# A residual block on one core: thirteen instead of nine column groups of the feed-forward projection are begun ahead, one product of each is kept in DRAM, and the operands made from the second half of the tokens come in another order

## The reference, cut to what matters

```python
x = x + rms_norm(mix, norm_post_mix[l])          # mix: two branches, merged, projected

h = rms_norm(x, norm_pre_ffn[l])
f = (jax.nn.silu(h @ w_ffn_gate[l]) * (h @ w_ffn_up[l])) @ w_ffn_down[l]
x = x + rms_norm(f, norm_post_ffn[l])
```

## Time and profile before

| what | value |
| --- | --- |
| median of 3 runs | 1701.26 us (1701.11 to 1701.61) |
| profiled execution, its own time | 1703.39 us |
| profiled execution, span from first to last instruction | 1701.3 us |
| PE busy | 1626.9 us (96%) |
| POOL busy | 1305.1 us (77%) |
| DVE busy | 1002.7 us (59%) |
| mean granted TensorE clock | 0.98 |

### The profile page before, as it was taken

How to read it: one execution, slowest core, us unless ns; L and a number is a source line. 1 busy time by engine, 2 the same in 40 slices (tenths; PEclk the granted TensorE clock), 3 DMA queues, 4 the chain that set the end, 5 groups by cost and what they waited for, 6 DMA issues and landing times.

```text
span 1701.3 us, 24101 instructions
## 1 busy us (share of the span) xinstructions
PE 1626.9 (96%) x7328; PEld 1333.4 (78%) x7328; DVE 1002.7 (59%) x1148; ACT 567.9 (33%) x1065; POOL 1305.1 (77%) x1300
## 2 busy tenths in 40 slices
PE   8899999999999999999999967999999999999995
PEld 6677888888888778888888756788888887888884
DVE  5799736642177997666522679787555557215503
ACT  4577535442236775255322323101001013102000
POOL 5699976777787999867777755887777776778874
PEclk8999999999999999999999988999999999999997
DMA  4433433233354343522333451232222222734531
GB/s 145 118 99 111 118 104 88 74 96 98 94 149 118 103 112 108 169 75 79 93 93 97 139 183 44 84 103 87 69 62 68 74 62 60 239 95 139 190 110 59
DMA packets 113357, 178.89 MB, mean 105 GB/s; under 512 B 12672, under 2 KB 41600, under 8 KB 113280
## 3 DMA queue, kind: packets, MB, share of 16 engines
q1 hardware_dynamic: 90816, 135.97, 27.8%
q10 hardware_dynamic: 22464, 41.95, 7.4%
HBM read 157.42 MB, written 14.16 MB: 101 GB/s over the span
## 4 chain that ended last, share of the span: by engine, by line
PE 77%; POOL 12%; DVE 5%; issue 4%; ACT 2%; ACTq 0%; DMA 0%; POOLq 0%; SPq 0%; DVEq 0%
PE ps L730 11%; PE ps L732 11%; PE ps L731 11%; PE ps L961 8%; PE ps L963 8%; PE ps L962 7%; POOL w_lo L610 6%; PE ps L1049 5%; PE ps L1050 5%; PE ps L1051 5%; POOL w_hi L607 4%; POOL w_hi L590 1%; PE ps L801 1%; PE ps L876 1%; PE ps L803 1%
## 5 line engine op out<-in xcount | busy, mean ns | idle before, releaser
L593 POOL TENSOR_TENSOR w_lo<-w_raw,w_hi 128x512 fp32r<-128x512 f32 (+2 forms) x376 | 461.1, 1226 | 31.4
L590 POOL TENSOR_SCALAR w_hi<-w_raw 128x512 fp32r<-128x512 f32 (+2 forms) x376 | 247.2, 657 | 191.9 <-PE ps L732 116.8
L730 PE MATMUL ps<-h_hi,w_hi 128*128 128x512 f32 x672 | 264.9, 394 | 11.5 <-POOL w_lo L610 9.0
L732 PE MATMUL ps<-h_hi,w_lo 128*128 128x512 f32 x672 | 263.6, 392 | 0.0
L731 PE MATMUL ps<-h_lo,w_hi 128*128 128x512 f32 x672 | 262.6, 391 | 0.0
L1643 DVE TENSOR_TENSOR acc<-acc,sq 128x512 f32<-128x512 f32 x55 | 56.9, 1035 | 186.7 <-ACT sq L1387 165.6
L610 POOL TENSOR_TENSOR w_lo<-w_raw,w_hi 128x512 fp32r<-128x512 f32 (+1 forms) x112 | 153.5, 1370 | 9.3
L730 PEld LDWEIGHTS ps<-h_hi,w_hi 128*128 128x128 f32 x672 | 126.4, 188 | 43.1 <-issue 13.1
L961 PE MATMUL ps<-t,w_hi 128*128 128x512 f32 x352 | 140.6, 399 | 10.3 <-issue 5.7
L732 PEld LDWEIGHTS ps<-h_hi,w_lo 128*128 128x128 f32 x672 | 126.2, 188 | 28.0
L731 PEld LDWEIGHTS ps<-h_lo,w_hi 128*128 128x128 f32 x672 | 126.2, 188 | 26.2
(11 more groups left out here) (321 smaller groups left out, 4027.1 us busy)
## 6 DMA issues: line engine op xcount, KB each, us to landing
w_raw<-w_f SPq DMA_DIRECT2D x80, 256.0 KB, 3.2
w_raw<-w_step SPq DMA_DIRECT2D x64, 256.0 KB, 2.7
w_raw<-w_b SPq DMA_DIRECT2D x64, 256.0 KB, 3.2
w_raw<-w_d SPq DMA_DIRECT2D x64, 256.0 KB, 2.7
w_raw<-w_a SPq DMA_DIRECT2D x96, 128.0 KB, 2.0
xs<-x_t ACTq DMA_DIRECT2D x32, 256.0 KB, 3.4
w_raw<-w_q SPq DMA_DIRECT2D x32, 256.0 KB, 3.2
w_raw<-w_o SPq DMA_DIRECT2D x32, 256.0 KB, 3.2
```

The source lines that it names most:

```text
L590: nc.gpsimd.tensor_scalar(w_hi[:, s, w], w_raw[:, s, w], 1.0, 0.0, ALU.mult, ALU.add).then_inc(w_hi_made, 1)
L593: nc.gpsimd.tensor_tensor(w_lo[:, s, w], w_raw[:, s, w], rd(w_hi[:, s, w]), ALU.subtract).then_inc(w_lo_made, 1)
L730: mm(out, w_hi[:, s, w], x_hi, start=(k == 0), stop=False)
L732: last = mm(out, w_lo[:, s, w], x_hi, start=False, stop=(k == total - 1))
```

## The change

- EARLY becomes 13: 26 products on h0 run ahead. The weights for them come through a ring of their own (`w_ring`, in the place of t2, from the fifth block on).
- The a11 product of each of the 13 groups goes from PSUM into one of two SBUF tiles and from there to DRAM (`p1_scratch`), issued by ACT behind the copy. SP loads it back two groups ahead of its use (`load_p1`), as the last load of its round.
- The residual tiles: the reciprocal of the norm is written to PSUM bank 4, the scaled row to bank 5, the squares to banks 6 and 7. The sum of row c - 1 is made after the addition of row c. The scaling to h reads bank 4 and takes the lower tiles first.
- The operands are made in the order b22, t3, t1, t2, t4, and the five products of groups 0 and 1 run in pairs in that order (`first_two`: s4, s3, s1, s2, a22 of each) over all eight banks. `weight_sums` of groups 0, 1 and 2 move with it.
- statistic 4 stands after the second early product, statistic 5 after the thirteenth.
- At the end of the projection the last group lies in banks 4 to 7, the down projection waits for group 20 instead, four tiles of f0 are split a group earlier, and only the last tile's split is left behind the last products.

```diff
 K2 = KD // 2
-EARLY = 9
+EARLY = 13
...
+FIRST_TWO = ["s4 0", "s4 1", "s3 0", "s3 1", "s1 0", "s1 1", "s2 0", "s2 1", "a22 0", "a22 1"]
...
+            def load_early(n, t, q):
+                i = n - N_MIX
+                if i < RING:
+                    sp_eng.wait_ge(w_lo_made, n - RING + 1)
+                elif i < 2 * RING:
+                    sp_eng.wait_ge(blocks_done, N_MIX)
                 else:
-                    sp_eng.wait_ge(w_lo_made, first_op(EARLY - 2) + 1)
+                    sp_eng.wait_ge(w_lo_made, n - RING + 1)
+                sp_eng.dma_start(early_raw(n), w_f[t, :, quarter[q]])\
+                    .then_inc((up_loaded if i < RING else up_ring_loaded)[i % RING], 16)
...
+            def load_p1(t):
+                if t < 2:
+                    sp_eng.wait_ge(p1_stored[0], 16 * ((EARLY + 1) // 2))
+                    sp_eng.wait_ge(p1_stored[1], 16 * (EARLY // 2))
                 else:
...
+                    sp_eng.wait_ge(c11_made, t - 1)
+                sp_eng.dma_start(p1_raw(t), p1_d[t]).then_inc(p1_loaded[t % 2], 16)
+
+            load_early(first_op(0), 0, 0)
+            for t in range(1, EARLY):
+                load_early(first_op(t), t, 0)
+                load_early(second_op(t - 1), t - 1, 1)
+                if t == 4:
+                    sp_eng.wait_ge(w_lo_made, N_MIX + RING)
+                    load_a21(0)
+                    load_a22(0)
+                    load_a11(0)
+                    load_a12(0)
+                if t == 9:
+                    load_a21(1)
+                    load_a12(1)
+                    sp_eng.wait_ge(added, 2 * KD)
+                    load_a22(1)
+                    load_a11(1)
+            load_early(second_op(EARLY - 1), EARLY - 1, 1)
+            load_p1(0)
+            load_p1(1)
...
+                if t < EARLY:
+                    load_p1(t)
...
+            for t in range(2):
+                split_sum("s4", t, 4, a11_raw(t))
+            for t in range(2):
+                split_sum("s3", t, 3, a21_raw(t))
+            for t in range(2):
+                split_sum("s1", t, 1, s1_raw(t))
+            for t in range(2):
+                split_sum("s2", t, 2, s2_raw(t))
+            for t in range(2):
+                split_a22(t)
...
+            def first_two():
+
+                pe.wait_ge(copied, 2 * EARLY)
+                for i, (name, x) in enumerate((("s4", x_b22), ("s3", x_t3), ("s1", x_t1), ("s2", x_t2))):
+                    pe.wait_ge(t_lo_made, K2 * (i + 1))
+                    for t in range(2):
+                        n = op_at(name, t)
+                        product(n, op_slot(n), x, 0, 4 * t + i)
+                pe.wait_ge(t_lo_made, 5 * K2)
+                n = op_at("a22", 0)
+                pe.wait_ge(u3_made, 1)
+                product(n, op_slot(n), x_t4, 0, 1)
+                pe.wait_ge(c12_made, 1)
+                product(n + 1, op_slot(n + 1), x_t4, 0, 0)
...
+                n = early_base(t)
+                banks = (2, 3, 1, 0) if t == 2 else [4 * (t % 2) + i for i in range(4)]
+                pe.wait_ge(c12_made, t - 1)
+                pe.wait_ge(c21_made, t - 1)
+                product(n, op_slot(n), x_t2, 0, banks[0])
+                product(n + 1, op_slot(n + 1), x_t1, 0, banks[1])
+                product(n + 2, op_slot(n + 2), x_t3, 0, banks[2])
+                if t == 2:
+                    pe.wait_ge(c21_made, 2)
+                product(n + 3, op_slot(n + 3), x_t4, 0, banks[3])
                 pe.wait_ge(u2_made, t + 1)
-                product(n + 4, op_slot(n + 4), x_b22, 0, bank)
+                product(n + 4, op_slot(n + 4), x_b22, 0, banks[0])
...
                 early(first_op(0), 0)
-                stat_sum(4)
                 for t in range(1, EARLY):
                     early(first_op(t), 0)
-                    if t == 5:
+                    if t == 1:
+                        stat_sum(4)
+                    early(second_op(t - 1), K2)
+                    if t == 6:
                         stat_sum(5)
-                    early(second_op(t - 1), K2)
                 early(second_op(EARLY - 1), K2)
-                for t in range(EARLY):
+                first_two()
+                for t in range(2, EARLY):
...
                 if h == 0:
-                    pe.wait_ge(c21_made, KF)
+                    pe.wait_ge(c12_made, KF - 1)
...
             def first_copy(t):
                 n = first_op(t)
                 act.wait_ge(blocks_done, n + 1)
-                fn(p1_of(t), ps[:, (n - N_MIX) % 3, :], ACT.Copy).then_inc(copied, 1)
+                if t > 1:
+                    act.wait_ge(p1_stored[t % 2], 16 * (t // 2))
+                fn(p1_raw(t), ps[:, (n - N_MIX) % 3, :], ACT.Copy).then_inc(copied, 1)
+                act.wait_ge(copied, n - N_MIX + 1)
+                act.dma_start(p1_d[t], p1_raw(t)).then_inc(p1_stored[t % 2], 16)
...
-                act.wait_ge(summed, sum_base(5) + c + 1)
-                fn(sq[:], rows[:, c, :], ACT.Square).then_inc(squared, 1)
+                if c > 1:
+                    act.wait_ge(summed, sum_base(5) + c)
+                fn(ps[:, 6 + c % 2, :], rows[:, c, :], ACT.Square).then_inc(squared, 1)
...
             second_copy(7)
+            first_copy(9)
+            for k in range(K2):
+                act.wait_ge(h1_made, k + 1)
+                fn(b22[:, 0, k, :], rows[:, K2 + k, :], ACT.Copy).then_inc(t_hi_made, 1)
+            second_copy(8)
+            first_copy(10)
+            second_copy(9)
+            for k in range(K2):
+                t_hi(t3_made, t3, t3_f, k)
+            first_copy(11)
+            second_copy(10)
+            first_copy(12)
             for k in range(K2):
                 t_hi(t1_made, t1, t1_f, k)
-            second_copy(8)
+            second_copy(11)
+            second_copy(12)
+            act.wait_ge(w_lo_made, op_at("s3", 1) + 1)
...
+            for t in range(EARLY):
                 gate_0(t)
+                gate_1(t)
+                f1_out(t)
...
+                if t == KF - 2:
+                    for k in range(K2):
+                        f0_split(k)
...
                 f0_split(k)
...
-            for k in range(2 * KD, KF):
+            for k in range(2 * KD, KF - 1):
                 f0_split(k)
             gate_1(t)
+            f0_split(KF - 1)
...
+            def invert_to_bank(n):
...
+                nc.vector.reciprocal(ps[:, 4, :], rstd_of(n)[:]).then_inc(rstd_made, 1)
+                dve.wait_ge(rstd_made, n + 1)
+
+            def scale_row(c):
+                if c:
+                    dve.wait_ge(added, KD + c)
+                stt(ps[:, 5, :], rows[:, c, :], col("g_post_mix", c), ps[:, 4, :], ALU.mult, ALU.mult)\
+                    .then_inc(scaled, 1)
+
+            def add_row(c):
+                dve.wait_ge(scaled, KD + c + 1)
+                dve.wait_ge(xs_loaded[c % 2], 16 * (4 * 4 + c // 2 + 1))
+                tt(rows[:, c, :], ps[:, 5, :], xs[:, c % 2, :], ALU.add).then_inc(added, 1)
+
+            def sum_row(c):
+                dve.wait_ge(squared, c + (sq_base(5) + 1))
+                dve.wait_ge(summed, sum_base(5) + c + 1)
+                tt(acc[:], ps[:, 6 + c % 2, :], acc[:], ALU.add).then_inc(summed, 1)
+
             open_sum(5)
-            dve.wait_ge(rstd_made, 5)
+            invert_to_bank(4)
             for c in range(KD):
-                add_norm(4, "g_post_mix", KD, 4, c // 2, c % 2)
-                add_square(5, c, (squared, c + (sq_base(5) + 1)))
+                scale_row(c)
+                add_row(c)
+                if c:
+                    sum_row(c - 1)
+            sum_row(KD - 1)
...
-            for t in range(KD):
-                stt(rows[:, t, :], rows[:, t, :], col("g_pre_ffn", t), rstd_b[:], ALU.mult, ALU.mult)\
+            for t in [*range(K2, KD), *range(K2)]:
+                stt(rows[:, t, :], rows[:, t, :], col("g_pre_ffn", t), ps[:, 4, :], ALU.mult, ALU.mult)\
                     .then_inc(h1_made, 1)
             for k in range(K2):
-                dve.wait_ge(h1_made, k + 1)
+                t_lo(0, b22, rows[:, K2 + k, :], k)
+            weight_sums(1)
+            for k in range(K2):
...
-                t_lo(3 * K2, t4, t4_f[:, 1, k, :], k)
+                t_lo(4 * K2, t4, t4_f[:, 1, k, :], k)
+            dve.wait_ge(copied, 2 * EARLY)
+            take_u2(0)
             take_u3(0)
+            take_c11(0)
+            take_u4(0)
             take_c22(0)
-            for k in range(K2):
-                t_lo(4 * K2, b22, rows[:, K2 + k, :], k)
-            weight_sums(1)
+            take_c12(0)
+            weight_sums(2)
             take_f0(0)
...
+                if t == KF - 2:
+                    for k in range(K2):
+                        f0_split(k)
...
-            for k in range(KD):
+            for k in range(K2, KD):
                 f0_split(k)
             take_u3(t)
+            for k in range(KD, KD + 2):
+                f0_split(k)
```

(7 more changed lines are left out.)

310 lines of the change are left out of this document (136 added, 174 removed).

## The result

| | before | after |
| --- | --- | --- |
| median | 1701.43 us (4 runs, 1701.11 to 1701.93) | **1681.04 us** (4 runs, 1679.05 to 1682.07) |
| profiled execution, span | 1701.3 us | 1680.3 us |
| mean granted clock | 0.98 | 0.988 |
| PE lost in the early stage and the pairs (972 to 1112) | 34.6 us | 17.8 us |
| PE lost at the down projection's start | 6.5 us | 2.1 us |

The ratio is 0.9872, 95% interval 0.9857 to 0.9887. The forecast was 1673, with 1662 to 1687 as its range. "Lost" is what the starts of PE's matmuls lie apart beyond 0.229 us each, summed over the stretch where they lie over 0.26 apart; the two gains, 16.8 and 4.4, are, to 0.2, the 21.0 by which the span fell.

What follows compares the result with a forecast made beforehand. PE lost 34.5 us between 972.0 and 1070.6, in the end waiting for DVE, whose SBUF-only instructions are stretched while POOL splits. From 1701.3, 22.5 gained there and 5.5 at the down projection gave 1673.3, so 1673 us; range 1662 to 1687.

Steps and rivals of the forecast that it cites:

- rival B: Operand chain longer: each SBUF-only DVE instruction waits for one whole POOL instruction, 1.57 us each; +8, 1681 us; chance 22%.
- the sign named on record: Forecast wrong if DVE's operand chain, 24 us from 1024 to 1048, has another length; each us moves the time by one.
- Statistic 4, rows through PSUM: Early stage: the wait of 2.3 us before statistic 4 goes; row instructions take 0.68 us each, 2.1 of DVE per row.
- Rival D: Residual rows: PSUM results or operands are stretched as SBUF ones are, rows stay at 5.1 us; +20, 1693 us; chance 8%.
- Statistic 5: Early stage: row 7 added at 1004.3, so PE's wait of 13.9 us before statistic 5 goes, at most 0.5 left.
- The chain of operands: DVE, b22's lo parts to t1: starts at 1024, mostly 1.24 us per instruction, t1 stands at 1048.
- The wait before the pairs: PE waits from 1045 to 1050 for copies behind t1's hi parts: 5.2 us, and 1.9 of clock.
- The backlog before group 3: After the pairs DVE owes two groups' results, so PE waits 3.0 us before group 3, and about 1.5 of clock.
- Spilled tiles: 13 stores and 13 loads of 256 KB; the loads, two groups ahead, cost zero if they land in time.
- Rival E: Groups: the spilled tile's load takes over 11 us and delays each group's sums; 1706 us at 3 us excess; chance 5%.
- Down projection: Start of the down projection: of 6.3 us lost to PE's wait for a22 and the low clock, 5.5 go.
- Rival C: Operand chain shorter: DVE and POOL interleave with less loss, the wait at 1045 and most backlog vanish; -8, 1665 us; chance 15%.

Runs made afterwards that it cites:

- e1: The changed kernel with the residual rows of the second half back in SBUF; 1688.11 us, against 1681.04 for the changed kernel.
- e2: The changed kernel with group 0's four weight loads moved from t = 4 to t = 8; 1682.68 us, against 1681.04.
- e8: The changed kernel without the stores and loads of p1, so its output is another; 1680.44 us, ratio 0.9857 to the kernel before.
- e4: The changed kernel with the down projection's start as it was before the change; 1685.72 us, against 1681.04.
- e6: The changed kernel with statistic 5 behind product 14 instead of product 12 on PE; 1675.52 us, ratio 0.9850 to the kernel before.
- e3: The changed kernel with ACT's copies of early products 24 and 25 ahead of t1's hi parts; 1678.46 us, against 1681.04.
- e7: The changed kernel with statistic 5 later, b22's hi parts earlier, and copies of products 21 to 25 ahead of or between t3's and t1's hi parts; 1676.14 us.

## Why the prediction was right, point by point

The sum had 12 us lost in the early stage and the pairs and 0.8 at the down projection, 12.8; measured were 17.8 and 2.1, 19.9. The 7.1 between them is the distance of the span from the forecast (1680.3 for 1673.3): 5.7 in steps 2 and 4 below, 2.9 less in step 5, 2.4 in step 6, 1.3 in step 8, and 0.5 of small ones. Of the 28.0 forecast 21.0 came, and at the places named. But the median came out at rival B's 1681 to the microsecond, and not by B's mechanism: that the range took it in, as B's price, was luck. Nor did the sign named on record catch it: the chain had its length of 24, and the time was still 7 off.

1. *Statistic 4, rows through PSUM.* Right: no wait before statistic 4, scale 0.75, addition 0.69, sum 0.68 (forecast 0.68 each). Rival D is out: a PSUM result is not stretched either.
2. *Statistic 5: the step that failed.* "x of row c+2 ... lands after 4.0" took the landing time from a stage with less traffic (984 to 1004: 197 GB/s before, 319 after), and SP's loads of groups 0 and 1 were put at nothing ("free") since POOL has them in time; x beside them was not asked for. It took 8.4 us for row 2 and 5.7 in the median, row 7 was added at 1009.9 instead of 1004.3, and PE waited 5.4 and ran twelve matmuls at 1.2 GHz behind it: 8.0 us for a forecast of at most 0.5. e1 shows that x, not DVE, sets the pace; e2 that the four weight loads of group 0 make the x loads beside them take 8.3 to 8.7 us, where the later ones of these two kernels take 4.1 to 5.8; e8 that without the spill the statistic is 3.6 us earlier (3.1 from the first early product on; e4, unedited there, is 1.7 earlier by the same count).
3. *The chain of operands.* Its length was right: 24 us from b22's first lo part to t1 by the forecast, 23.6 measured (1032.46 to 1056.06). In part that is luck: group 1's sums and t3 took 5.5 each for 4.0 and 5.0, and b22 lo, t3 lo and t1 made up for it with 4.3, 3.9 and 4.4 for 5.0 each, in part while POOL waited for PE. Its start was wrong, 1032.5 for 1024, since the copy of product 17, named in the forecast as what it stands behind, moved with PE's wait (e6).
4. *The wait before the pairs.* 5.2 and 1.9 of clock forecast; 3.0 without a fall of the clock, and 1.7 before product 24 for a forecast of 0.5. It was as named, ended by ACT's copy behind t1's hi parts (e3), and smaller only because PE itself came later by more than the copies did: its 26 products ended at 1054.7 for 1045, the copies at 1057.7 for 1050. Steps 2 and 4 together: forecast 7.6, measured 13.3.
5. *The backlog before group 3.* Forecast 3.0 and 1.5 of clock, measured 0.90 before group 2 and 0.24 before group 3, no clock. Over-sized by 2.9. DVE had been idle for 10.6 us before the pairs' first sum, so it owed nothing from before; why it then was through earlier than the sum had it was not looked into.
6. *A wait that was not in the sum*, 2.14 at 1071.16, ended by POOL; the section on the hardware has it.
7. *Spilled tiles.* Rival E is out: no wait of DVE between 1100 and 1400 is ended by such a load, which lands after 4.3 us (median; 6.1 at most).
8. *Down projection.* 5.5 forecast, 4.4 measured. The wait for the last group's sum went, as forecast; the 22nd split is late instead, against the earlier trace rows:

```profile
1430.18 0.50 PE L1103 MATMUL ps<-h_lo,w_hi 128*128 128x512 f32 x1 [1.75 <-DVE rows_r L2112]
```

Rival C is out as well, since the chain was not shorter. e7 comes near its time (a span of 1669.8) by another way, with the chain starting earlier at the same length.

## What to carry to other kernels

A landing time read in one stage holds for that stage's traffic; where a change makes the stage denser, ask of each burst of loads, though it is early for its own user, what else is issued beside it. If an edit that moves such a burst leaves the time as it is, look at each landing before calling the burst harmless: the delay can have moved along with it. An in-order queue that serves two masters (here ACT: copies for PE, hi parts for DVE) carries the wait of the one into the chain of the other, so ask of each long wait whose work is queued behind the instruction that ends it: the three moves of e7 were worth 7.0 us, a third of what the whole change had brought. And where runs of one kernel differ by 6 us, compare stages by the starts of their instructions, not whole times.
